# Three down slabs at the end of a feed-forward, a signal for each tile pair, and squares summed two tiles later

## What is computed

```python
def conv_ffn(h, w_up, conv_w, conv_b, w_down):
    u = h @ w_up                                   # 1024 -> 2 * 2816
    up = jnp.pad(u, ((0, 0), (CONV_W - 1, 0), (0, 0)))
    u = sum(up[:, j:j + seq] * conv_w[j] for j in range(CONV_W)) + conv_b
    a, b = u[..., :D_FF], u[..., D_FF:]
    return (jax.nn.silu(a) * b) @ w_down           # 2816 -> 1024

for i in range(DEPTH):                             # DEPTH = 2
    h = rms_norm(x, norm_mix_g[i])
    x = x + mixer_i(h)
    x = x + conv_ffn(rms_norm(x, norm_ffn_g[i]), ...)
# third block
x = x + gate_m * hybrid_mixer(...)
h = rmsnorm(x, norm_mlp_w[i]) * (1.0 + scale_f) + shift_f
x = x + gate_f * (jnp.square(jax.nn.relu(h @ w_up[i])) @ w_down[i])
return rmsnorm(x, norm_final_w)
```

## Time and profile before

| | |
|---|---|
| median of 3 runs | 1426.47 us (1426.31 to 1426.48) |
| profiled execution | 1428.68 us, its span 1426.7 us |
| TensorE busy | 1323.8 us, 93% |
| VectorE busy | 954.2 us, 67% |
| ScalarE busy | 720.8 us, 51% |
| granted TensorE clock, mean | 0.951 |
| loads of weight slabs | 381 of 512 KB, 3.7 us each to landing |

### The profile page before, as it was taken

One profiled execution on the slowest core, in us unless ns is written; L12 is line 12 of the kernel. 1 busy time (PEld: TensorE's weight loads), 2 busy tenths in 40 slices (PEclk: granted clock), 3 DMA queues, 4 the chain that ended last, 5 costly groups with the idle time before them and its releaser, 6 DMA issues.

```text
span 1426.7 us, 27583 instructions
## 1 busy us (share of the span) xinstructions
PE 1323.8 (93%) x10064; PEld 1268.9 (89%) x10064; DVE 954.2 (67%) x1668; ACT 720.8 (51%) x1138; POOL 25.7 (2%) x52
## 2 busy tenths in 40 slices
PE   6877799999899999889999889999999999899997
PEld 6866799999798889889999878888889999899997
DVE  4574678888678876768888684765757555555554
ACT  4334365555545455345555464655655434544442
POOL 0000000000000000100000000000000000000000
PEclk9879899999899999989999879999999999799998
DMA  6303655555267655845555423323324554355540
GB/s 257 125 0 127 213 165 189 177 176 186 99 231 259 220 205 211 284 156 183 178 187 187 140 89 104 133 99 123 118 104 148 187 187 157 118 177 178 188 164 30
DMA packets 63223, 230.31 MB, mean 161 GB/s; under 512 B 6976, under 2 KB 7104, under 8 KB 63040
## 3 DMA queue, kind: packets, MB, share of 16 engines
q1 hardware_dynamic: 56256, 204.40, 41.9%
q0 software_dynamic: 6912, 25.17, 5.1%
HBM read 228.49 MB, written 1.05 MB: 161 GB/s over the span
## 4 chain that ended last, share of the span: by engine, by line
PE 73%; DVE 14%; ACT 6%; issue 4%; DMA 3%; DVEq 0%; ACTq 0%; SPq 0%; POOL 0%; PEldq 0%; POOLq 0%
PE ps L184 22%; PE ps L185 21%; PE ps L186 21%; DVE w_lo L176 4%; ACT w_hi L171 2%; DMA arena<-ada 2%; DVE arena L337 2%; PE ps L213 2%; PE ps L1197 1%; PE ps L1206 1%; PE ps L1196 1%; DVE arena L1011 1%; ACT sq L271 0%; PE ps L1144 0%; PE ps L891 0%
## 5 line engine op out<-in xcount | busy, mean ns | idle before, releaser
L176 DVE TENSOR_TENSOR w_lo<-w_raw,w_hi 128x1024 fp32r<-128x1024 f32 x381 | 463.0, 1221 | 168.3 <-ACT w_hi L171 167.2
L184 PE MATMUL ps<-a_hi,w_hi 128*128 128x256 f32 x1912 | 563.9, 295 | 11.5 <-DVE a_lo L1055 5.3
L185 PE MATMUL ps<-a_lo,w_hi 128*128 128x256 f32 x1912 | 550.4, 288 | 0.0
L186 PE MATMUL ps<-a_hi,w_lo 128*128 128x256 f32 x1912 | 549.9, 288 | 0.0
L184 PEld LDWEIGHTS ps<-a_hi,w_hi 128*128 128x128 f32 x1912 | 376.4, 197 | 25.7 <-issue 18.5
L171 ACT ACTIVATE w_hi<-w_raw 128x1024 fp32r<-128x1024 f32 x381 | 387.1, 1046 | 18.9 <-PE ps L186 12.6
L185 PEld LDWEIGHTS ps<-a_lo,w_hi 128*128 128x128 f32 x1912 | 377.2, 197 | 0.6 <-issue 0.2
L186 PEld LDWEIGHTS ps<-a_hi,w_lo 128*128 128x128 f32 x1912 | 376.6, 197 | 0.0
L184 PE MATMUL ps<-b_hi,w_hi 128*128 128x256 f32 x928 | 267.5, 288 | 20.7 <-DVE w_lo L176 11.4
L185 PE MATMUL ps<-b_lo,w_hi 128*128 128x256 f32 x928 | 265.6, 286 | 0.0
L186 PE MATMUL ps<-b_hi,w_lo 128*128 128x256 f32 x928 | 265.4, 286 | 0.0
(11 more groups left out here) (254 smaller groups left out, 1269.4 us busy)
## 6 DMA issues: line engine op xcount, KB each, us to landing
w_raw<-stream SPq DMA_DIRECT2D x381, 512.0 KB, 3.7
arena<-ada POOLq DMA_DIRECT2D x48, 512.0 KB, 4.7
con<-consts SPq DMA_DIRECT2D x1, 1440.0 KB, 12.7
arena<-x SPq DMA_DIRECT2D x1, 1024.0 KB, 4.9
out<-arena SPq DMA_DIRECT2D x2, 512.0 KB, 3.0
arena<-c_rows SPq DMA_DIRECT2D x1, 512.0 KB, 3.5
par<-params SPq DMA_DIRECT2D x1, 319.0 KB, 5.2
con<-consts SPq DMA_DIRECT2D x1, 193.0 KB, 2.4
```

What stands on the lines that cost most here:

```text
L176: dve.tensor_tensor(w_lo[:, s % RING], w_raw[:, s % RING], w_hi[:, s % RING].bitcast(F32), ALU.subtract).then_inc(w_lo_ready, 1)
L184: pe.matmul(o, wh, xh, start=start, stop=False, skip_group_check=shared)
L185: pe.matmul(o, wh, xl, start=False, stop=False, skip_group_check=shared)
L186: return pe.matmul(o, wl, xh, start=False, stop=stop, skip_group_check=shared)
```

## The change

The order of the feed-forward's end becomes up 20, up 21, down 19, down 20, down 21; SP takes the three slabs in question from other places of the stream (`late`), with its load ranges cut there. One turn of TensorE's loop is written out instead. `hi` of the last pair waits for down 19, whose buffer it takes. In the last down slab of each of the three chains, tiles 1, 3 and 5 increment `down_done`, and the adds wait for their own pair of tiles (the last one for the slab). The squares behind the three chains are made for two tiles in one instruction. `operand_and_sums` sums tile k - 2 where it summed tile k, and the last two tiles are summed at the beginning of the second slab. The diff, cut to its core:

```diff
+        down_done = sem("down_done")
@@ down_slab
+                if last and m in (1, 3, 5):
+                    mm.then_inc(down_done, 1)
             mm.then_inc(w_used, 1)
+
+        def sum_ready_wait(dve, end, j, used):
+
+            if j < 3:
+                dve.wait_ge(down_done, 3 * end + j + 1)
+            else:
+                dve.wait_ge(w_used, used)
@@ operand_and_sums
             def each(k):
                 pe.wait_ge(a_ready, NT * v + k + 1)
-                sum_squares(pe, v, k)
+                if k >= 2:
+                    sum_squares(pe, v, k - 2)
+            return each
+
+        def last_sums(pe, v):
+
+            def each(k):
+                if k == 0:
+                    sum_squares(pe, v, NT - 2)
+                    sum_squares(pe, v, NT - 1)
             return each
+        def act_prep_pair(act, v, j, g):
+
+            for m in (2 * j, 2 * j + 1):
+                if g:
+                    act.wait_ge(res_ready, NT * v + m + 1)
+                    act.activation(a_hi[:, m], res[:, m], ACT.Copy, scale=pcol(g, m)).then_inc(a_hi_ready, 1)
+            act.wait_ge(res_ready, NT * v + 2 * j + 2)
+            act.activation(sq[:, 2 * j:2 * j + 2], res[:, 2 * j:2 * j + 2], ACT.Square).then_inc(sq_ready, 2)
@@ attention_pe
-            slab_gemm(pe, 1, ps[:, 1, 0:SEQ], a_hi, a_lo)
+            slab_gemm(pe, 1, ps[:, 1, 0:SEQ], a_hi, a_lo, each=last_sums(pe, 0))
@@ ffn_pe
-            up_pair(0, s0, each=operand_and_sums(pe, v))
+            up_pair(0, s0, each=(operand_and_sums(pe, v), last_sums(pe, v)))
-            with pe.Fori(0, (FF_PAIRS - 2) // UNROLL) as it:
+            with pe.Fori(0, LATER) as it:
                 for u in range(UNROLL):
                     up_pair(2 + u, s0 + 5 + 3 * u, it, 3 * UNROLL)
                     down(1 + u, s0 + 7 + 3 * u, it, 3 * UNROLL)
-            down(FF_PAIRS - 1, s0 + 3 * FF_PAIRS - 1)
+            for p in range(2 + UNROLL * LATER, FF_PAIRS - 2):
+                up_pair(p, s0 + 3 * p - 1)
+                down(p - 1, s0 + 3 * p + 1)
+            up_pair(FF_PAIRS - 2, s0 + 3 * FF_PAIRS - 7)
+            up_pair(FF_PAIRS - 1, s0 + 3 * FF_PAIRS - 5)
+            for n in (3, 2, 1):
+                down(FF_PAIRS - n, s0 + 3 * FF_PAIRS - n)
@@ ffn_act
-                hi(p, s - 6 + 3, it)
+                hi(p, s0 + 3 * FF_PAIRS - 2 if p == FF_PAIRS - 1 else s, it)
-            for m in range(NT):
-                if next_gain:
-                    act_prep(act, v + 1, m, next_gain)
-                else:
-                    square(act, v + 1, m)
+            for j in range(NT // 2):
+                act_prep_pair(act, v + 1, j, next_gain)
@@ ffn_vec
-                evict(p, 0, s, it, ds)
+                used = s - 1 if p == FF_PAIRS - 1 else s
+                evict(p, 0, used, it, ds)
@@ add_down
-            dve.wait_ge(w_used, used)
             for j in range(NT // 2):
+                sum_ready_wait(dve, end, j, used)
@@ mlp_act
-            for m in range(NT):
-                square(act, 6, m)
+            for j in range(NT // 2):
+                act_prep_pair(act, 6, j, None)
@@ mlp_vec
-            dve.wait_ge(w_used, SLABS)
             for m in range(NT):
+                sum_ready_wait(dve, ENDS[2], m // 2, SLABS)
@@ sync
+            late = {}
+            for s0 in (S_FFN0, S_FFN1):
+                s = s0 + 3 * FF_PAIRS
+                late.update({s - 5: s - 4, s - 4: s - 3, s - 3: s - 5})
-                src = stream[s] if it is None else ...
+                src = stream[late.get(s, s)] if it is None else ...
```

## The result

The changed kernel takes 1432.74 us (median of 20 runs, 1426.75 to 1440.95). The kernel before, run beside it, takes 1427.97 us (20 runs, 1426.31 to 1432.33). The ratio is 1.0033, with a 95% interval of 1.0018 to 1.0048: slower, by 2.6 to 6.9 us. The forecast was 4.6 us faster, and 1432.74 lies outside the range.

What follows compares the result with a forecast made beforehand. TensorE's product lines were taken as the bound, 64% of the span. Waits for `b_lo` -1.8, tails -5.9 and starts +3.1 gave -4.6 us, a median of 1421.9 us, range 1417.8 to 1425.6.

Steps and rivals of the forecast that it cites:

- The rest: SP's reordered loads, the written-out TensorE loop turn and written-out first pairs: taken as 0, far end 1.3 us each.
- the three ends: Ends of both feed-forwards and the MLP, where chains of down products finish: gains of 1.8 and 5.9 us, together 7.7.
- The `b_lo` wait: TensorE's wait before the last down slab of each feed-forward: reordering gains 0.9 us each, bounds 0.7 and 1.4.
- The tails: From last down slab to variance, earlier adds and paired squares gain 2.4, 2.4 and 1.1 us, sum 5.9.
- T: Start of the last down slab's first product; variance forecast at T + 9.2 and T + 7.4, before T + 11.5 and T + 9.9.
- Rival D: Clock falls as the down slab ends, all 32 sums at low pace: 4.2 us slower, 1430.7 us; chance 0.06.
- The starts: Sums two tiles later at three starts cost 1.3 us per feed-forward and 0.5 at attention, sum 3.1.
- The larger case named there: Both feed-forward starts at their upper bound, 2.0 us each, by the skill's clock rule: total -3.2 us, 1423.3.
- The base: Median of the kernel before that the forecast started from: 1426.47 us.

Runs made afterwards that it cites:

- h1: Kernel before with only one turn of TensorE's loop in each feed-forward written out, old order kept: median 1437.73 us, ratio 1.0034.
- i1: Changed kernel whole, but TensorE's loop has nine turns of two pairs, so no turn is written out: 1426.05 us, ratio 0.9963 against before.
- h3: Kernel before with the order edit of the down slabs alone and a TensorE loop of nine turns of two pairs: ratio 0.9989.
- e1: Changed kernel with 46 of the 48 `ada` loads cut to 8 KB each: 1417.86 us, ratio 0.9892 against before.
- e2: Kernel before with 46 of the 48 `ada` loads cut to 8 KB each: 1421.61 us, ratio 0.9914 against before.
- g3: Changed kernel, sums in old places, `ada` dot products at steps 0, 2, 4, 6, 8, 9 of a head: 1420.07 us, ratio 0.9898 against before.
- i2: g3 with TensorE's loop as nine turns of two pairs, no turn written out: 1417.65 us, ratio 0.9907 against before.
- g1: Kernel before with the new order of the last three down slabs alone, including the written-out turn it needs: 1434.91 us, ratio 1.0016.
- g2: Kernel before with the signals a tile pair, earlier adds and paired squares alone: 1424.41 us, ratio 0.9932.
- f3: Changed kernel, sums in old places, 46 of the 48 `ada` loads cut to 8 KB each: 1412.53 us, ratio 0.9866 against before.
- e4: Kernel before with only the sums of squares moved two tiles later: ratio 1.0016.

## Why the prediction was wrong

**The step that failed** is in "The rest": "One loop turn of TensorE is written out: the same instructions, fetched once more", costed at nothing, with one wait of 1.3 us as its far end. By itself it costs 4.9 us (h1, 2.0 to 7.7). In the whole change it decides the sign: the ratio is 1.0033 and 1.0020 with it, 0.9963 without it (i1), some 8 to 10 us; the intervals overlap, so that it costs more there than by itself isn't shown. The way, as the runs show it: the longer program, weight loads 0.2 us later in every stage of after and h1 against before and h3 (even from 60 to 170 us, far ahead of the turn: 3.4 against 3.1 in after and before), `ada` loads 5.3 to 5.7 us instead of 4.8 to 5.2, VectorE's waits for them 17 to 23 us instead of 7 to 14 (all with the dot products in their old places), and products at the low clock behind a long wait (0.51 behind 454.20). Two kinds of experiment cut this way off at the `ada` loads, small loads (e1 against e2) and more room between the dot products (g3 against i2), and each takes the loss away. The forecast looked for loads among TensorE's waits at the three ends only, and no rival of it had a load that lands later. The waits for `ada` were in the trace of before, and even in its chain of waits with 2%; I didn't ask what they would cost if a load came later.

**Not shown** is why the loads land later. It isn't the traffic of the fetches: from 900 to 1200 us both kernels run the same loops, and from 840 to 1240 both fetch 14 packets. Whether it is the length as such, or where program and data come to lie with it, no run here tells; between 36 and 41 packets there was no kernel. The Trainium skill, Runtime: NRT & Kernel Launch, section Instruction fetch mechanics, says that instructions are fetched in blocks of 16 KiB and that this is mostly hidden. The block's size agrees (0.67 MB / 41 packets = 16 KB), and neither h1 nor after shows a wait of TensorE in the first feed-forward that before hasn't (a start of 2.0 us and the one for `b_lo`); the later landings are no part of what that section describes.

**The `b_lo` wait.** Forecast 0.9 us each, with the product behind it still 0.5 late through VectorE's own chain. Found: a start 0.32 late in the first (366.29 behind 365.85, pitch 0.12; 0.16 of it idle) and 0.28 in the second (822.98 behind 822.58). From spread to spread, the order alone (g1) saves 200.45 - 199.05 = 1.4 us (bound 1.4) and 198.82 - 196.59 = 2.2 us. The second figure is less sure than it looks, since that stage takes 198.0 to 199.3 us in kernels without an edit in it, where the first takes 200.1 to 200.5. Direction right, sized too small: the two down slabs in front cover VectorE's chain almost whole.

**The tails.** First feed-forward: -2.4 as forecast (T + 9.1 against T + 9.2): ScalarE's pairs hold TensorE up until the last eight sums, and these go at the low pace (1.82 us, where the three groups before took 1.05). Second: T + 6.7 against T + 7.4, because the clock stayed at 1.00 for all 32 sums; MLP: 3.75 us from the last product to the end of the sums against 5.28, so -1.5 where -1.1 was taken; from spread to spread it is -1.9. Rival D, the early fall of the clock, didn't come. Signals and pairs alone (g2) save 2.0, 2.5 and 1.8 us in the three stages, 6.3 against 5.9. All ends together (f3, g3 and i2 against before) save 3.6, 4.4 and 1.9. That is 9.8 by the stages, 9.0 by those of f3 against e2 and 9.1 by their medians, where the sum had 7.7.

**The starts.** The mechanism was right (sixteen sums behind the wait, at 0.50), the size was not: 5.3 us by f3 against e1, where 3.1 was taken; e4 shows 2.3 (-0.7 to 5.3). Between e1 and f3 the two feed-forwards lose 2.0 and 2.4 before the spread, and win back 1.2 and 1.3 behind it, so the 1.3 each was, if anything, high. e4, the later sums without the new ends, shows no such win: its feed-forwards take 200.29 and 198.57 us. For the attention start, e1's second spread (56.94) stands 1.7 us behind that of f3 (55.27), but this point scatters: it lies at 55.3 to 56.6 us in the fifteen kernels with the sums in their old places and at 56.0 to 56.9 in the five with the later ones, on average 0.5 later, which is what was taken. Another 2.4 lie in the third block, between spreads that no edit touches; that stretch took about 392.4, 393.9, 394.9 or 396.8 us in kernels of every kind (396.78 before, 392.46 after), so this part may be its scatter. (By these spans the difference is 5.8, by the medians 5.3.) What the starts cost is therefore not known better than some 2 to 5 us. The Trainium skill, TensorE: Matmul & The Clock Gate, section HAM oscillation, says that idle between bursts is paid again in half-rate products: the 0.51 behind 454.20 agrees, since 448.0 to 450.0 still had 1.00. The 0.50 behind 171.40 doesn't bear it out, though the forecast read it so: the clock was at 0.50 from 162.0 on, ahead of that wait. The larger case named there (2.0 each) is what the spreads show before the win behind them is taken off.

**The base.** The forecast took 1426.47 us, three runs. The set beside the changed kernel has 1427.97, so that 1.5 us of the miss of 10.8 are the base and the rest is the change, +4.8 in place of -4.6. The six sets of the kernel before have medians of 1427.97 to 1433.91: a range of 8 us for an absolute time is hard to meet when the base alone moves by 6. i1 shows it, whose gain came out as forecast and whose 1426.05 us still lie outside.

## What to carry to other kernels

Before an edit is costed at nothing because it executes the same instructions, look whether it makes the program longer, and compare the least landing of a plain load (in the view of its tile) and the instruction packets (on the page) before and after: two lines that show a shift that no engine's row shows. A wait of VectorE for a load inside a chain grows as soon as anything makes that load later, and TensorE then waits with it. Look for such waits of 1 us in the trace of before and give them room first: here that alone was worth 7 us, nearly as much as the whole tuning of the ends (9 us). And take the length of a stage from several executions before two traces are compared stage by stage: 243.0 and 250.9 us were the same program.

## What the runs showed of the hardware

- A longer TensorE program (41 instead of 36 instruction packets of 16 KB) goes with loads of 512 KB landing 0.2 us later, throughout the execution: 3.2 to 3.3 against 3.0 to 3.1 us at the least, eight kernels against twelve. Its mechanism is open.
- A loop of nine turns of two pairs costs nothing that shows against one of four turns of four pairs with two pairs written out: 199.07 us (h3) and 199.05 (g1) for the first feed-forward. For the second it is 197.15 and 196.59, within what that stage scatters by (1.3 us).
- 32 sums of one column directly behind the products of the second feed-forward went at the high pace to their end (3.63 us), 3.7 us behind the last product. Before, with a gap in front of them, the clock was 1.00 up to 813.1 and 0.50 behind it.
- A wait of TensorE of 4.11 us was followed by 4.8 us at 0.51 (the clock fell within the wait, near 452): the head was 6.5 us longer, the wait and half of it again.
